# Cross attention with keys and queries projected by tokens, turned by 32x32 squares and transfers

## What is computed

```python
x   = x + rmsnorm(mixer_out, g_post_mix)       # residual after the mixer
h   = rmsnorm(x, g_pre_cross)                  # 256 tokens x 1024
m   = rmsnorm(mem_2, g_mem)                    # 256 memory tokens x 1024
k,v = split(m @ w_ckv_2)                       # 1024 and 1024 columns, 4 heads x 256
q   = h @ w_cq_2                               # 1024 columns, 4 heads x 256
p   = softmax(q k^T * 256 ** -0.5)             # per head
x   = x + rmsnorm((p v) @ w_co_2, g_post_cross)
```

## Time and profile before

| | |
|---|---|
| median of 3 runs | 1419.28 us (1418.56 to 1419.42) |
| profiled execution, own time | 1418.27 us |
| its span | 1416.5 us |
| TensorE (PE) busy | 1403.6 us, 99% |
| VectorE (DVE) busy | 857.3 us, 61% |
| ScalarE (ACT) busy | 704.9 us, 50% |
| GpSimd (POOL) busy | 259.8 us, 18% |
| granted TensorE clock | 0.999 |

### The profile page before, as it was taken

How to read it: one execution, slowest core, us unless ns; L and a number is a source line. 1 busy time by engine, 2 the same in 40 slices (tenths; PEclk the granted TensorE clock), 3 DMA queues, 4 the chain that set the end, 5 groups by cost and what they waited for, 6 DMA issues and landing times.

```text
span 1416.5 us, 18653 instructions
## 1 busy us (share of the span) xinstructions
PE 1403.6 (99%) x7200; PEld 1190.3 (84%) x7200; DVE 857.3 (61%) x1035; ACT 704.9 (50%) x981; POOL 259.8 (18%) x504
## 2 busy tenths in 40 slices
PE   9999999999999999999999999999999999999998
PEld 7888889988888888888889888888887989888886
DVE  5656565756555565555656565555796655565554
ACT  6554454445444454444555555444555554644443
POOL 1022210002222222222012113222201100132222
PEclk9999999999999999999999999999999999999999
DMA  9765654455655656665544446665553553366562
GB/s 349 290 213 201 219 186 156 166 185 192 221 201 198 218 196 215 207 220 198 180 149 150 139 168 258 216 222 200 186 177 136 188 179 134 125 228 225 197 220 74
DMA packets 71655, 275.55 MB, mean 195 GB/s; under 512 B 17392, under 2 KB 37232, under 8 KB 40848
## 3 DMA queue, kind: packets, MB, share of 16 engines
q1 hardware_dynamic: 57168, 259.57, 51.6%
q0 software_dynamic: 14400, 14.81, 3.4%
HBM read 259.88 MB, written 1.05 MB: 184 GB/s over the span
## 4 chain that ended last, share of the span: by engine, by line
PE 95%; ACT 2%; DVE 1%; issue 1%; DMA 0%; POOL 0%; SPq 0%; DVEq 0%; POOLq 0%; ACTq 0%
PE prod L1140 16%; PE prod L1141 16%; PE prod L1144 15%; PE acc L1144 10%; PE acc L1140 10%; PE acc L1141 10%; PE prod L1134 5%; PE prod L1136 5%; PE prod L1135 5%; PE acc L1338 1%; PE acc L1159 1%; ACT w_hi L1493 1%; PE acc L1358 1%; DVE w_lo L1743 0%; PE o_bank L1394 0%
## 5 line engine op out<-in xcount | busy, mean ns | idle before, releaser
L1743 DVE TENSOR_TENSOR w_lo<-raw,w_hi 128x2048 fp32r<-128x2048 f32 x233 | 533.6, 2291 | 383.4 <-ACT w_hi L1493 380.8
L1493 ACT CAST w_hi<-raw 128x2048 fp32r<-128x2048 f32 x233 | 444.2, 1907 | 431.6 <-PE prod L1144 182.1
L1140 PE MATMUL prod<-w_hi,acts_h 128*128 128x512 f32 x944 | 370.2, 392 | 2.5 <-DVE w_lo L1752 1.8
L1144 PE MATMUL prod<-w_hi,acts_l 128*128 128x512 f32 x944 | 367.7, 389 | 0.0
L1141 PE MATMUL prod<-w_lo,acts_h 128*128 128x512 f32 x944 | 367.4, 389 | 0.0
L1004 POOL DMA_DIRECT2D four<-four x408 | 200.1, 498 | 602.4 <-DVE four L1904 585.3
L1140 PE MATMUL acc<-w_hi,mix_h 128*128 128x512 f32 x600 | 236.0, 393 | 0.0
L1144 PE MATMUL acc<-w_hi,mix_l 128*128 128x512 f32 x600 | 233.7, 390 | 0.0
L1141 PE MATMUL acc<-w_lo,mix_h 128*128 128x512 f32 x600 | 233.5, 389 | 0.0
L1140 PEld LDWEIGHTS prod<-w_hi,acts_h 128*128 128x128 f32 x944 | 177.2, 188 | 43.0 <-issue 6.9
L1144 PEld LDWEIGHTS prod<-w_hi,acts_l 128*128 128x128 f32 x944 | 177.2, 188 | 37.5 <-DVE acts_l L1814 0.3
(11 more groups left out here) (277 smaller groups left out, 1261.7 us busy)
## 6 DMA issues: line engine op xcount, KB each, us to landing
raw<-in_weights_dram SPq DMA_DIRECT2D x234, 1024.0 KB, 5.0
four<-four SPq DMA_DIRECT2D x408, 16.0 KB, 2.1
four<-four POOLq DMA_DIRECT2D x408, 16.0 KB, 1.9
raw<-in_weights_dram SPq DMA_DIRECT2D x16, 256.0 KB, 6.9
work<-in_mem_dram POOLq DMA_DIRECT2D x2, 1024.0 KB, 13.5
grow<-in_gain_rows_dram POOLq DMA_DIRECT2D x4, 512.0 KB, 3.7
tabs<-in_tabs_dram POOLq DMA_DIRECT2D x1, 1632.0 KB, 9.9
work<-in_x_t_dram SPq DMA_DIRECT2D x4, 256.0 KB, 5.7
```

The costliest lines, as they stand in the source:

```text
L1140: pe.matmul(out, still_hi, wh, start=first, stop=False, skip_group_check=True)
L1144: return pe.matmul(out, still_lo, wh, start=False, stop=last, skip_group_check=True)
L1493: act.copy(w_hi[:, c % RING], raw[:, c % RAW]).then_inc(hi_done, 1)
L1743: dve.tensor_tensor(w_lo[:, c % RING], raw[:, c % RAW], w_hi[:, c % RING].bitcast(F32), ALU.subtract).then_inc(lo_done, 1)
```

## The change

Keys and queries are projected by `project_turned`, which makes the same two `rows_half` chunks as `project_tokens` for 512 features. ScalarE copies the banks into a buffer in cut order, VectorE transposes 128 x 1024 in 32x32 squares into a second buffer, and 16 transfers (8 on SyncE, 8 on POOL) carry them to `mem_k` or `q`. There the element of token i in tile k stands at steps of 8 elements, and the score matmuls read queries and keys with that step. `spread` goes; POOL instead multiplies the per-token factor by the score scale (`scales`). The order becomes: keys (4 chunks), `prep`, first values (2), queries (4) with the first score behind them, last values (2) with three ticks among them, `w_co_2`. The first `mem_prep` moves behind the first `w_out_2` chunk.

```diff
 class Plan:
+    def project_turned(self, source, col, dest, at, buffers, of="x", mid=None, between=None, scales=None):
+        for k_half in range(2):
+            self.chunk("rows_half", (*source, "half", (k_half, col)), mid, e=self.e, k_half=k_half, dest=dest, at=at,
+                       of=of, acts=self.acts if of == "x" else self.mem, free=self.bank_free(2), turned=self.turned,
+                       buffers=buffers, scales=scales)
...
+        self.turn_behind[self.c + RAW] = self.items[-1]
+        self.turned += 1
+        for t in range(2):
+            self.bank_reader.append(("cut_done", 2 * self.turned - 1 + t))
+        self.e += 2
...
 make_plan:
-    pl.mem_prep("g_mem", [4, 5, 6, 7], [8, 9, 10, 11], "mem2")
     pl.add("scale_x", stat=pl.stat)
...
     downs(slot, "w_out_2", 0, order,
-          lambda n: n == 1 and pl.mem_prep("g_mem", [0, 1, 2, 3], [4, 5, 6, 7], "mem2"))
+          lambda n: n < 2 and pl.mem_prep("g_mem", *(([4, 5, 6, 7], [8, 9, 10, 11]), ([0, 1, 2, 3], [4, 5, 6, 7]))[n],
+                                          "mem2"))
...
-    for n in range(4):
-        pl.project(("w_ckv_2", 0), n * COLS, "mem_k", 2 * n, of="mem2")
+    for n in range(2):
+        pl.project_turned(("w_ckv_2", 0), 512 * n, "mem_k", 4 * n, "cross", of="mem2")
     pl.prep("g_pre_cross", "post", wait=True)
-    for n in range(2):
-        pl.project_tokens(("w_ckv_2", 0), D + 512 * n, "mem_v", 512 * n, of="mem2")
-    pl.spread("x")
+    query_scale = pl.scales([(2 * P) ** -0.5])
...
-    for n in range(4):
-        pl.project(("w_cq_2", 0), n * COLS, "q", 2 * n, mid=slot if n else None, factors=((2 * P) ** -0.5,) * 2)
-        if n:
-            end(slot)
-        pl.ready(units[n:n + 1])
-        pl.ready_v(units[n:n + 1])
+    pl.project_tokens(("w_ckv_2", 0), D, "mem_v", 0, of="mem2")
+    pl.ready_v(units[0:2])
+    pl.project_turned(("w_cq_2", 0), 0, "q", 0, "cross", scales=query_scale)
+    pl.ready(units[0:2])
+    pl.project_turned(("w_cq_2", 0), 512, "q", 4, "cross", scales=query_scale)
+    end(slot)
+    pl.project_tokens(("w_ckv_2", 0), D + 512, "mem_v", 512, of="mem2", mid=slot, between=lambda: end(slot))
+    pl.ready(units[2:4])
+    pl.ready_v(units[2:4])
+    end(slot)
     pl.draining = True
     downs(slot, "w_co_2", 0, pairs_of(0, 1, 2, 3))
...
 layout and transfers:
+        def in_tokens(name, tile):
+            four_tiles = dests[name][:, tile // 4 * 4:tile // 4 * 4 + 4].rearrange("p a b -> p (a b)")
+            return four_tiles.rearrange("p (i t k) -> p k t i", t=2, k=4)[:, tile % 4]
...
+        def move_features(engine, it, token_blocks, done):
+            to = dests[it["dest"]][:, it["at"]:it["at"] + 4].rearrange("p a b -> p (a b)")
+            engine.wait_ge(features_turned, it["turned"] + 1)
+            for a in token_blocks:
+                for b in range(4):
+                    engine.dma_start(to[32 * b:32 * b + 32, a * S:(a + 1) * S],
+                                     cut_buffer(it, 1)[32 * a:32 * a + 32, b * S:(b + 1) * S]
+                                     ).then_inc(done, 16)
...
 SyncE, behind the load of chunk c:
+                if c in plan.turn_behind:
+                    move_features(sp, plan.turn_behind[c], (0, 1), early_features_moved)
 POOL:
+                elif kind == "rows_half" and it["k_half"] and it.get("turned") is not None:
+                    move_features(pool, it, (2, 3), late_features_moved)
 TensorE, scores:
+                    if unit["moved"]:
+                        pe.wait_ge(early_features_moved, 128 * unit["moved"])
+                        pe.wait_ge(late_features_moved, 128 * unit["moved"])
...
-                                mm = pe.matmul(bank[:, at:at + width], dests[q][r0:r1, qt + n, t * P:(t + 1) * P],
-                                               dests[k][r0:r1, kt + n, 0:width], start=(n == 0),
-                                               stop=(n == unit["tiles"] - 1))
+                                mm = pe.matmul(bank[:, at:at + width],
+                                               tokens_of(q, unit["q_blocks"], slice(r0, r1), qt + n, t),
+                                               keys_of(k, unit["k_blocks"], slice(r0, r1), kt + n, width),
+                                               start=(n == 0), stop=(n == unit["tiles"] - 1))
 ScalarE, turned rows_half:
+                            to, source = cut_tokens(it, t), in_cut_order(prod_flat[(it["e"] + t) % 2])
+                            if len(columns_of) == 1:
+                                ins = act.activation(to, source, ACT.Copy, scale=columns_of[0][:, t:t + 1])
...
+                            ins.then_inc(cut_done, 1)
 VectorE, turned rows_half:
+                        dve.wait_ge(cut_done, 2 * it["turned"] + 2)
+                        if it["turned"]:
+                            dve.wait_ge(early_features_moved, 128 * it["turned"])
+                            dve.wait_ge(late_features_moved, 128 * it["turned"])
+                        dve.transpose(cut_buffer(it, 1).rearrange("p (b i n) -> p b n i", b=4, n=8),
+                                      cut_buffer(it, 0).rearrange("p (b n j) -> p b n j", b=4, n=8)
+                                      ).then_inc(features_turned, 1)
```

More of the change, by code:

```diff
@@ L337, in project_tokens, with scales @@
             self.e += 2
+    def project_turned(self, source, col, dest, at, buffers, of="x", mid=None, between=None, scales=None):
[3 more added lines that the diff above has]
+                       buffers=buffers, scales=scales)
+            self.used(of)
+            if between and k_half == 0:
+                between()
+        self.turn_behind[self.c + RAW] = self.items[-1]
[3 more added lines that the diff above has]
+        self.e += 2
+    def scales(self, factors):
+        at = self.n_scales
+        self.n_scales += len(factors)
+        self.add("scales", factors=factors, at=at, stat=self.stat)
+        return list(range(at, at + len(factors)))
     def ticks(self, groups):
@@ L806, in build @@
         rb = sb("rb", [P, 2, S])
+        scales = sb("scales", [P, 16])
         stats = sb("stats", [P, 22])
@@ L969, in group_bank, with cut_buffer, cut_tokens, in_cut_order @@
             return (prod[it["e"] % 2], prod[(it["e"] + 1) % 2], aux[:].rearrange("p (a b) -> p a b", a=2), o_bank)[g]
+        cut_buffers = {"pool": (obuf[:, 0:4], sq[:, 0:4]), "diff": (mem_k[:, 0:4], obuf[:, 0:4]),
+                       "cross": (k_t[:, 0:4], k_t[:, 4:8])}
+        def cut_buffer(it, n):
+            return cut_buffers[it["buffers"]][n].rearrange("p a b -> p (a b)")
+        def cut_tokens(it, t):
+            return cut_buffer(it, 0).rearrange("p (b t k j) -> p t k b j", b=4, t=2, k=4)[:, t]
+        def in_cut_order(ap):
+            return ap.rearrange("p (k b j) -> p k b j", k=4, b=4)
+        def in_tokens(name, tile):
+            four_tiles = dests[name][:, tile // 4 * 4:tile // 4 * 4 + 4].rearrange("p a b -> p (a b)")
+            return four_tiles.rearrange("p (i t k) -> p k t i", t=2, k=4)[:, tile % 4]
+        def keys_of(name, blocks, rows, tile, width):
+            if not blocks:
+                return dests[name][rows, tile, 0:width]
+            if width == P:
+                return in_tokens(name, tile)[rows, 0]
+            return in_tokens(name, tile)[rows]
+        def tokens_of(name, blocks, rows, tile, t):
+            if not blocks:
+                return dests[name][rows, tile, t * P:(t + 1) * P]
+            return in_tokens(name, tile)[rows, t]
+        def move_features(engine, it, token_blocks, done):
[6 more added lines that the diff above has]
+                                     ).then_inc(done, 16)
         def reader(engine, told):
@@ L1100, in _ @@
                     move_blocks(pool, (2, 3), late_blocks_moved)
+                elif kind == "rows_half" and it["k_half"] and it.get("turned") is not None:
+                    move_features(pool, it, (2, 3), late_features_moved)
+                elif kind == "scales":
+                    pool.wait_ge(rstd_done, it["stat"])
+                    for n, factor in enumerate(it["factors"]):
+                        ins = pool.tensor_scalar(scales[:, 2 * (it["at"] + n):2 * (it["at"] + n) + 2], rstd["x"], factor,
+                                                 None, ALU.mult)
+                    ins.then_inc(scales_done, len(it["factors"]))
                 elif kind == "load_mem2":
@@ L1549, in _ @@
                                            scale=rstd["x"][:, t:t + 1]).then_inc(gated, 1)
+                    elif kind == "rows_half" and it["k_half"] and it.get("turned") is not None:
+                        if it["scales"]:
+                            act.wait_ge(scales_done, it["scales"][-1] + 1)
+                            columns_of = [scales[:, 2 * n:2 * n + 2] for n in it["scales"]]
+                        else:
+                            act.wait_ge(rstd_done, it["stat"])
```

(22 more changed lines are left out.)

26 lines of the change are left out of this document (18 added, 8 removed).

## The result

| | before | changed |
|---|---|---|
| median | 1419.35 us (4 runs) | 1426.11 us (1425.61 to 1426.66, 4 runs) |
| profiled execution, own time | 1418.27 us | 1426.37 us |
| its span | 1416.5 us | 1424.6 us |

The ratio is 1.0050, with a 95% interval of 1.0034 to 1.0065: the changed kernel is slower by 6.8 us. The forecast was 1418.5 us and no change.

A forecast was written before the change was run, and what follows sets the result against it. TensorE, busy for 99% of the span, was taken as the bound. Terms -2.3 - 0.4 - 0.9 + 1.4 + 1.25 + 0.2 = -0.75 us gave about 1418.5 us from 1419.28, no change; range 1415.6 to 1422.6.

The forecast's parts named there:

- Chunk form: Cross attention projections: four key and four query chunks go from 5.76 to 5.47 us each, -2.3 us.
- `spread`, and the wait at the output step: Four small matmuls go, -0.4 us; TensorE's wait for VectorE's low part at L1379 goes as memory work leaves `rg`, -0.9 us.
- `mem_prep` behind the first `w_out_2` chunk: Memory work there delays VectorE's split and `head_scale`, so TensorE waits at `head_turn`: +1.4 us, between 0 and 2.
- The key exchange ahead of the residual: VectorE's cut-copy wait and 1.24 us transpose delay the residual pieces, so TensorE waits before turning x: +1.25 us.
- the rival in which the step costs VectorE alone: Transpose with stepped writes takes twice its time, +1.1 us, 1419.6 us, still no change; chance 0.10.
- The exchange: Key transfers land 9.2 us after their projection; the first score wants them at 10.9 us, so TensorE loses nothing.
- The one late load foreseen: Weight load queued behind SyncE's eight issues: ScalarE wants it at 10.9 us, gets it near 12.3, long before TensorE needs it.
- Third head ahead of `w_co_2`: That chunk waits for the head's exponentials, 3.65 us against TensorE's 3.45 us of work: +0.2 us, between 0 and 1.
- Score operands: Sixteen cross-attention score matmuls read at a 32-byte step; two clocks a column was taken as slack, so no cost.
- The bound set beside it: Upper limit for the stepped score matmuls: twice their time, 4 x 1.73 = 6.9 us.
- reading with steps costs TensorE: Rival: the 32-byte step halves the score stream, +6.9 us, 1425.4 us, slower; chance 0.16.

## Why the prediction was wrong, point by point

- **Chunk form** (-2.3 us): right, 5.46 to 5.48 us a chunk for the 5.47 forecast.
- **`spread`, and the wait at the output step** (-0.4 and -0.9): right, both gone.
- **`mem_prep` behind the first `w_out_2` chunk** (+1.4): right in mechanism and place, 1.25 us. The timeline of VectorE in the changed kernel reads like the sum: memory work, the split put off, `head_scale`, at which TensorE's wait ends. The row that answers to 1107.04 of the earlier trace rows has no idle time left before it; the last row is TensorE's `head_turn` with its wait:

```profile
1104.12 1.68 DVE L2116 SCALAR_TENSOR_TENSOR mix_l<-obuf,vecs,mix_h 128x256 fp32r<-128x256 f32 x4 [3.21 <-ACT mix_h L1782]
1105.72 2.28 DVE L1857 TENSOR_TENSOR w_lo<-raw,w_hi 128x2048 fp32r<-128x2048 f32 x1
1107.92 0.60 DVE L2199 SCALAR_TENSOR_TENSOR sq<-prod,head_stats,work 128x128 f32<-128x128 f32 x2
...
1108.58 0.65 PE L1558 MATMUL aux<-tabs,sq 128*128 128x128 f32 x4 [1.25 <-DVE sq L2199]
```

- **The key exchange ahead of the residual** (+1.25): right in mechanism, 1.6 us. The transpose was mis-sized: 2.04 to 2.20 us with its stepped writes, 1.245 us without them (the 1.24 worked out). With plain writes the wait is 0.9 us, so that the estimate of the rest was 0.4 us too high. (By that same working a transpose of twice the time makes 2.5 us, not the 2.3 written there.) The rival in which the step costs VectorE alone held as to VectorE.
- **The exchange** (0): right, no score waited for a transfer, since the list of TensorE's waits has none. The one late load foreseen, that of the first `w_co_2` chunk, shows as a wait of ScalarE, and TensorE saw none of it:

```profile
1180.51 1.90 ACT L1579 CAST w_hi<-raw 128x2048 fp32r<-128x2048 f32 x1 [1.37 <-DMA raw<-in_weights_dram]
```

- **Third head ahead of `w_co_2`** (+0.2): right, 0.2 us.
- **Score operands** (0): this is the step that failed. The prediction argued that scores "draw elements at half the rate that a stream without steps sustains here, so half the reading rate would still do". They cost 7.8 us. The rate was read from the output columns of a record and taken for the rate of reading; the run with stepped values shows a score record priced as 512 columns, twice its own, and the step doubled the scores as it doubled the values. Why a record without a step takes two clocks a column stays open. The bound set beside it, 6.9 us, was exceeded too, since a stepped record takes 2.13 times a plain one (0.461 by 0.216 us).

So the rival "reading with steps costs TensorE", given 0.16 and 1425.4 us, is what happened: 1426.11 us. The stretch grew by 7.7 us where that rival's sum had 6.15 (6.9 - 0.75): the scores cost 0.9 us more than its price, and the stepped transpose, which that sum left out, 0.7 us. Without steps the remaining terms came to -1.0 us in the stretch where -0.75 was forecast. As measured one by one they add up to -1.3 us, so the place of a few tenths stays open.

## What to carry to other kernels

Price a layout by who reads it: a streamed operand of TensorE whose neighbours lie 16 or 32 bytes apart took about twice its time here, while the same step on the loaded operand was nearly hidden. Where an exchange must leave some order behind, give runs to the streamed operand and let the transfers or the loaded operand bear the rest. And when a bound rests on a rate read from a profile, ask whether the engine reads as often as the record counts columns, and measure one matmul with the step before the sum relies on it. Two waits of about 1 us each were removed here by a change of order alone, once the traces had named the work in front of them.

## What was not expected of the hardware

The price sets in somewhere between 8 and 16 bytes: at 8 bytes a head's scores took 1.81 us, at 16 bytes 3.66 to 3.75, at 32 bytes 3.68 (1.73 without one). VectorE's transpose pays in its writes as TensorE does in its reads, 2.04 to 2.20 us against 1.245. Transfers in runs of 128 bytes in place of 1024 cost TensorE nothing in these runs: it waited for neither.
